# Feed forward's second projection of a three-layer network: seven block products in place of eight

## The reference

```
m = concatenate([a, b]) @ w_out
h = h + rmsnorm(m, post_mix_g)
f = rmsnorm(h, pre_ff_g) @ w_ff1          # 512 x 1024 @ 1024 x 4096
f = square(relu(f)) @ w_ff2               # 512 x 4096 @ 4096 x 1024
h = h + rmsnorm(f, post_ff_g)
```

## Time and profile before

| | us |
|---|---|
| median of 3 runs | 1731.29 |
| lowest, highest | 1729.97, 1731.40 |
| the profiled execution, its time | 1730.73 |
| its span, first to last instruction | 1729.0 |
| PE busy in the span | 1715.3 (99%) |
| VectorE, ScalarE, GpSimd busy | 1209.1, 820.2, 46.4 |

### The profile page before, as it was taken

How to read it: one execution, slowest core, us unless ns; L and a number is a source line. 1 busy time by engine, 2 the same in 40 slices (tenths; PEclk the granted TensorE clock), 3 DMA queues, 4 the chain that set the end, 5 groups by cost and what they waited for, 6 DMA issues and landing times.

```text
span 1729.0 us, 26320 instructions
## 1 busy us (share of the span) xinstructions
PE 1715.3 (99%) x10458; PEld 1497.2 (87%) x10458; DVE 1209.1 (70%) x1975; ACT 820.2 (47%) x1449; POOL 46.4 (3%) x103
## 2 busy tenths in 40 slices
PE   9999999999999999999999999999999999999998
PEld 8777788999999887777989999989888898999997
DVE  4588787777787735666877777868446876677776
ACT  4477744444445235664444444443565555333342
POOL 0212000000000000000000000000000000000000
PEclk9999999999999999999999999999999999999999
DMA  8343332333334232224133333352314224333331
GB/s 276 113 134 118 119 89 87 109 98 110 101 99 153 86 105 84 81 91 122 39 103 98 110 110 97 99 165 82 110 44 140 63 73 126 106 98 98 100 109 49
DMA packets 220125, 181.36 MB, mean 105 GB/s; under 512 B 9906, under 2 KB 178771, under 8 KB 220003
## 3 DMA queue, kind: packets, MB, share of 16 engines
q1 hardware_dynamic: 217954, 175.48, 33.1%
q0 software_dynamic: 2048, 4.20, 0.9%
HBM read 173.32 MB, written 7.38 MB: 105 GB/s over the span
## 4 chain that ended last, share of the span: by engine, by line
PE 93%; DVE 4%; ACT 1%; DMA 1%; issue 1%; POOL 0%; DVEq 0%; POOLq 0%
PE ps L733 29%; PE ps L734 28%; PE ps L735 28%; PE ps L1092 1%; PE ps L1137 1%; PE ps L1163 1%; PE ps L1112 1%; PE ps L1151 1%; DMA arena<-arena 1%; PE ps L987 1%; DVE wlo L1701 0%; DVE xl L1793 0%; PE ps L1102 0%; PE ps L972 0%; ACT whi L1321 0%
## 5 line engine op out<-in xcount | busy, mean ns | idle before, releaser
L1701 DVE TENSOR_TENSOR wlo<-raw,whi 128x1024 fp32r<-128x1024 f32 (+1 forms) x276 | 317.6, 1167 | 181.3 <-ACT whi L1321 181.0
L733 PE MATMUL ps<-xh,whi 128*128 128x256 f32 (+1 forms) x1016 | 332.4, 327 | 2.3 <-DVE xl L1793 2.3
L735 PE MATMUL ps<-xh,wlo 128*128 128x256 f32 (+1 forms) x1016 | 326.1, 321 | 0.0
L734 PE MATMUL ps<-xl,whi 128*128 128x256 f32 (+1 forms) x1016 | 325.9, 321 | 0.0
L1321 ACT ACTIVATE whi<-raw 128x1024 fp32r<-128x1024 f32 (+1 forms) x276 | 274.6, 1007 | 80.9 <-DMA raw<-in_w_ff 36.4
L733 PE MATMUL ps<-whi,hh 128*128 128x512 f32 x728 | 288.7, 397 | 1.4 <-DVE wlo L1701 1.3
L734 PE MATMUL ps<-wlo,hh 128*128 128x512 f32 x728 | 285.2, 392 | 0.0
L735 PE MATMUL ps<-whi,hl 128*128 128x512 f32 x728 | 283.6, 390 | 0.0
L733 PEld LDWEIGHTS ps<-xh,whi 128*128 128x128 f32 x1016 | 194.1, 191 | 25.8 <-issue 8.8
L735 PEld LDWEIGHTS ps<-xh,wlo 128*128 128x128 f32 x1016 | 194.1, 191 | 14.4
L734 PEld LDWEIGHTS ps<-xl,whi 128*128 128x128 f32 x1016 | 194.4, 191 | 12.2
(11 more groups left out here) (272 smaller groups left out, 2935.3 us busy)
## 6 DMA issues: line engine op xcount, KB each, us to landing
raw<-in_ffn_w_in SPq DMA_DIRECT2D x88, 512.0 KB, 3.8
raw<-in_w_ff SPq DMA_DIRECT2D x64, 512.0 KB, 4.2
raw<-in_ffn_w_out SPq DMA_DIRECT2D x44, 512.0 KB, 3.9
raw<-in_a_w_qkv SPq DMA_DIRECT2D x22, 512.0 KB, 5.5
raw<-in_w_in SPq DMA_DIRECT2D x20, 512.0 KB, 3.8
raw<-in_kv_w SPq DMA_DIRECT2D x16, 512.0 KB, 4.1
bias_skewed<-bias_rows SPq DMA_DIRECT2D x8, 640.0 KB
arena<-arena POOLq DMA_DIRECT2D x64, 64.0 KB, 2.7
```

The source lines that it names most:

```text
L733: e.matmul(o, ah, bh, start=start, stop=False, **more)
L734: e.matmul(o, ah, bl, start=False, stop=False, **more)
L735: return e.matmul(o, al, bh, start=False, stop=stop, **more)
L1701: e.tensor_tensor(lo[:, 0:n], src, f32(hi[:, 0:n]), ALU.subtract).then_inc(s.lo, 1)
```

## The change

**The second projection.** Groups 1 to 6 are no longer 16 pieces but a 2 x 2 block product by seven products: tokens in two halves of 256, the four hidden blocks in two halves, outputs in two halves of 512. Each product has two pieces (two token tiles of 128), so a group has 14 pieces. The left operands are three quarters of the hidden blocks as they are and four sums of quarters; the right ones are quarters of the weights and sums of them. Two chains of products run on in PSUM banks that are held: `SEVEN` says for every product which chain it adds to, whether it starts it, and into which token half m and output half nh its running sum is sent, with which sign. After each piece ScalarE copies the bank (times the sign) to one of four buffers, and GpSimd's queue issues a transfer that adds the buffer onto `mb`. PE may add to the bank again when it has been copied.

**Operands.** The hidden blocks of these groups are kept unsplit in the storage of `hh` (`hidden_words`). VectorE makes the left sums, ScalarE the high and VectorE the low part of each left operand, in `left` steps two products ahead. The right operands are loaded by SP into the four buffers of `x`; their sums are made by accumulating transfers from DRAM, issued by GpSimd. `x` is therefore parked in DRAM before and loaded back after. A group has four such sums on right operands and 14 additions onto `mb`.

**Weights.** All weight tiles are laid out in DRAM as the kernel reads them: every load of a tile is 128 contiguous pieces of 4 KB. The right operands have a table of their own, `c_row_tiles`.

**Smaller edits.** `FEED_PIECES` is "2212" in place of "2222". The scratch for GpSimd's transfer descriptors goes from 1024 to 2048. `tri`, the triangle of ones, moves into the arena and is loaded before the gate. The last gain vector has a place of its own, and semaphores with one use are merged into others.

```diff
-FEED_PIECES = ["1111"] + ["2222"] * 13
+FEED_PIECES = ["1111"] + ["2212"] * 13
+SEVEN_FIRST, SEVEN_LAST = 1, 6
+SEVEN = [("a11", 0, True, 0, 0, 1), ("a12", 1, True, 0, 0, 1), ("s1", 1, True, 1, 1, -1), ("s4", 1, False, 0, 1, -1),
+         ("s2", 0, False, 0, 1, -1), ("s3", 0, False, 1, 1, -1), ("a22", 0, False, 1, 0, 1)]
...
+    def seven(self, g):
...
+        rights = [Right(a, ("load", landed), [(a, "a", (first, 1))]), Right(b, ("load", b_need), (), b_next),
+                  Right(a, ("a", 48 * turn + 16), [(a, "a", (last, 1))]),
+                  Right(c, ("load", c_need), [(d, "d", (last, 1))], c_next),
+                  Right(a, ("a", 48 * turn + 32), [(a, "a", (last, 0))]), Right(d, ("d", 16 * turn + 16), (), d_next),
+                  Right(a, ("a", 48 * turn + 48), (), following)]
...
+        for n, (name, chain, start, m, nh, sign) in enumerate(SEVEN):
+            u = 7 * (g - SEVEN_FIRST) + n
+            unit = self.unit("seven", rights[n], None)
+            if g == SEVEN_LAST and n == 6:
+                self.step("gain", self.fifth)
+                self.step("unpark", unit)
+            for t in range(2):
...
+                self.step("seven", piece)
...
+                self.step("seven_post", piece)
+                if t == 1:
+                    self.left(u + 2)
+                yield
...
# PE
+            elif what == "seven":
+                p, = arg
+                b, c = p.bank, slice(p.t * 128, p.t * 128 + 128)
+                wh, wl = self.weight(p.unit, 2)
+                lh, ll = self.left_parts(self.plan.entry_of[p.u])
+                w.wait_ge(s.lo, p.unit + 1)
+                w.wait_ge(s.left_lo, p.u + 1)
+                if p.before is None:
+                    w.wait_ge(*freed[b])
+                else:
+                    w.wait_ge(s.evicted, p.before + 1)
+                for k in (0, 1):
+                    m = mm3(e, ps[b][:], lh[:, k, c], ll[:, k, c], wh[:, k, :], wl[:, k, :], p.start and k == 0, k == 1,
+                            skip_group_check=True)
+                m.then_inc(s.rows, 1)
# ACT
+            elif what == "seven_post":
+                p, = arg
+                w.wait_ge(s.rows, p.value)
+                if p.sent >= 4:
+                    w.wait_ge(s.added[p.sent % 4], 16 * (p.sent // 4))
+                e.activation(self.evict_to(p.sent), ps[p.bank][:], ACT.Copy, scale=float(p.sign)).then_inc(s.evicted, 1)
# DVE
+            elif what == "left_sum":
...
+                if name == "s1":
+                    e.tensor_tensor(tmp, a22, a21, ALU.subtract).then_inc(s.left_sum, 1)
+                elif name == "s2":
+                    e.scalar_tensor_tensor(tmp, tmp, -1.0, a11, ALU.mult, ALU.subtract).then_inc(s.left_sum, 1)
+                elif name == "s4":
+                    e.scalar_tensor_tensor(a12, a12, -1.0, tmp, ALU.mult, ALU.subtract).then_inc(s.left_sum, 1)
+                else:
+                    e.tensor_tensor(a21, a11, a21, ALU.subtract).then_inc(s.left_sum, 1)
# POOL
+            elif what == "split" and self.plan.units[arg[0]][0] == "seven":
+                m, = arg
+                right = self.plan.units[m][1]
+                for buffer, chain, source in right.sums:
+                    if chain == "a":
+                        w.wait_ge(s.lo, m + 1)
+                    else:
+                        w.wait_ge(s.right[buffer], right.before)
+                    e.dma_start(self.x[:, buffer, :], self.row_tile(*source),
+                                accum_op=ALU.add).then_inc(s.right_sum[chain], 16)
+            elif what == "seven_post":
+                p, = arg
+                w.wait_ge(s.evicted, p.sent + 1)
+                w.wait_ge(s.mb, 16)
+                if p.earlier is not None:
+                    w.wait_ge(s.added[p.earlier % 4], 16 * (p.earlier // 4 + 1))
+                e.dma_start(self.mb[:, p.tile, p.nh * 512:p.nh * 512 + 512], self.evict_to(p.sent), accum_op=ALU.add).then_inc(s.added[p.sent % 4], 16)
# SP
+            e.dma_start(self.raw[:, m % RAW, :], ap["c_tiles"][m]).then_inc(s.raw[m % RAW], 16)
...
+            elif what == "park":
+                w.wait_ge(s.add, 8)
+                for t in range(4):
+                    e.dma_start(self.parked[t * 128:t * 128 + 128, :], self.x[:, t, :]).then_inc(s.x, 16)
+            elif what == "seven_load":
+                w.wait_ge(s.x, 128)
+                w.wait_ge(s.y, 16)
+                for buffer, source in ((1, (4, 0)), (2, (6, 0)), (3, (6, 1)), (0, (8, 0))):
+                    rows_load(buffer, source)
...
-    nc = _bacc.Bacc("TRN2", target_bir_lowering=False, num_devices=1, dynamic_dma_scratch_size=1024)
+    nc = _bacc.Bacc("TRN2", target_bir_lowering=False, num_devices=1, dynamic_dma_scratch_size=2048)
```

More of the change, by code:

```diff
@@ L61, in __init__ @@
         self.kind, self.nh, self.t, self.bank, self.i = kind, nh, t, bank, i
-        self.norm, self.group, self.value = norm, group, None
+        self.norm, self.group, self.value, self.added = norm, group, None, None
+class Piece:
+    def __init__(self, u, unit, t, bank, start, before, value, tile, nh, sign, sent, earlier):
+        self.u, self.unit, self.t, self.bank, self.start, self.before, self.value = u, unit, t, bank, start, before, value
+        self.tile, self.nh, self.sign, self.sent, self.earlier = tile, nh, sign, sent, earlier
+class Right:
+    def __init__(self, buffer, need, sums=(), load=None):
+        self.buffer, self.need, self.sums, self.load, self.before = buffer, need, sums, load, None
 class Pair:
-    def __init__(self, kind, n, table, columns, blocks):
+    def __init__(self, kind, n, table, columns, blocks, first=None):
         self.kind, self.table, self.columns, self.blocks = kind, table, columns, blocks
@@ L942, in unsplit @@
             return self.raw[:, tile % RAW, :], 1024
+        if kind == "seven":
+            return self.x[:, tile.buffer, :], 1024
         if kind == "s2":
@@ L1314, in scalar @@
                     w.wait_ge(s.raw[tile % RAW], self.raw_at[tile])
+                elif kind == "seven":
+                    what, value = tile.need
+                    w.wait_ge(s.right[tile.buffer] if what == "load" else s.right_sum[what], value)
                 else:
@@ L1754, in vector @@
                 for i, k in enumerate(pair.blocks):
+                    if pair.kind == "relu":
+                        for n in range(14 * (SEVEN_LAST - SEVEN_FIRST) - 4, 14 * (SEVEN_LAST - SEVEN_FIRST)):
+                            w.wait_ge(s.added[n % 4], 16 * (n // 4 + 1))
                     w.wait_ge(s.hh, pair.hidden[i] + 1)
@@ L2259, in sync @@
                 m, = arg
-                _, _, tile = self.plan.units[m]
+                kind, right, tile = self.plan.units[m]
+                if kind == "seven" and right.load is not None:
+                    w.wait_ge(s.hi, m + 1)
+                    w.wait_ge(s.lo, m + 1)
+                    rows_load(*right.load)
                 if tile is not None and tile + RAW < len(self.plan.tiles):
```

343 lines of the change are left out of this document (244 added, 99 removed).

## The result

| us | before | after |
|---|---|---|
| median of 3 runs | 1731.29 | 1739.84 |
| lowest, highest | 1729.97, 1731.40 | 1736.82, 1743.04 |
| forecast for after | | 1716.0 (1712 to 1729) |

The ratio is 1.0056, with a 95% interval of 1.0042 to 1.0069: the kernel became slower by 0.4 to 0.7%, and the forecast was 24 us too low. The sign was wrong too.

The account below looks back on a forecast made before the run. The prediction took PE's (TensorE's) work to bound the kernel: 1730.73 us less 16.5 for fewer pieces plus 1.5 for entry and exit gives 1715.7, put at 1716 us for the median, range 1712 to 1729.

Parts of the forecast that it names:

- The sign: Whole kernel: faster than before by over 0.2%, under 1727.8 us, chance 0.76.
- PE's work, -16.5 us: Second projection, groups 1 to 6: 14 pieces in place of 16, 2.75 us less per group, 16.5 us in all.
- Accumulate at the copy's price: DMA engines: adding transfers priced like copies, with the tiles 33 to 35 us of a 39.3 us group.
- Rival C: GpSimd's queue and DMA engines, 1430 to 1660 us: accumulating transfers become the bound; 1753 us at 1.5 times copy; chance 0.18.
- I take 0 for the steady state: Groups 1 to 6: engines' queue order costs PE 0 us, bounds 0 and 18 us.
- The wait of 2 us on ScalarE: s2's right operand: its sum takes 8 to 9 us, so ScalarE may stand 2 us, only one eviction behind it.
- Rival B: In-order queues take part back, VectorE and ScalarE waiting on each other: 1722 us, reaching 1719 to 1727.8; chance 0.20.
- Entry and exit, 1.5 together: Parking x, loading right operands and bringing x back: 1.5 us together, bounds 0 and 6.
- Layout 0: Weight tiles in DRAM: shorter landings but no gain, at best the 3.6 us PE waits for low parts.
- Scratch "buys no time that this trace shows": GpSimd's descriptor scratch, enlarged: no time gained that the trace of the kernel before shows.
- GpSimd's issue at 1 us: GpSimd's queue: 1 us to issue each of the 18 accumulating transfers per group.
- VectorE 33.2 and ScalarE 29.4 us per group: Busy time in a 39.3 us group of the second projection: VectorE 84%, ScalarE 75%, neither full.

Follow-up runs that it names:

- e12: Kernel after without its 108 adding transfers, with s3's left sum earlier and the last pair's high parts one step later: 1713.81 us, ratio 0.9905.
- e13: Kernel after with both order moves of e12 and all 108 GpSimd transfers plain, overwriting instead of adding: 1717.71 us, ratio 0.9927.
- e11: e6 with the right operand sum for s2 made by VectorE instead of an adding transfer, whole network computed: 1723.39 us, ratio 0.9958.
- e6: Kernel after, whole network, with s3's left sum earlier and the last pair's high parts one step later on ScalarE: 1731.67 us, ratio 1.0003.
- e15: Kernel after, whole network, with only s3's left sum made earlier, together with those of s2 and s4: 1731.31 us, ratio 1.0003.
- e9: Kernel after in its own order, with none of its 108 adding transfers: 1721.68 us, ratio 0.9949.
- e4: Kernel before with only the weight tiles laid out in DRAM as in the kernel after: 1729.56 us, ratio 0.9997.
- e3: Kernel after without the 84 transfers onto the result, the 24 adding ones on right operands kept: 1726.85 us, ratio 0.9981.
- e8: Kernel after with the descriptor scratch of 1024 as before: 1747.97 us, ratio 1.0101.
- e7: e6 with two right operand sums per group (for s2 and d's operand) made by GpSimd's own addition: 1746.06 us, ratio 1.0086.

## Why the prediction was wrong, point by point

- **PE's work, -16.5 us: right.** e12 and e13 reach 1713.8 and 1717.7 us.
- **"Accumulate at the copy's price": the failed step.** It measured 1.91 times the copy. The 5.8 MB of a group are 32 us of engine time and not the 17 of e13's copies (the forecast had 19 to 21); with 12 to 14 for the tiles that is 44 to 46, the share of 1.05 to 1.09 of the windows. The forecast's 33 to 35 us at the copy's price is near what e13 shows (a share of 0.74 to 0.78, which is 29 to 31 us of 39.3). Rival C had the right factor, by a rule that I cited and gave too small a chance (0.18), but its formula was wrong: it made the period follow the engines' share (1817 us at 2), and e11 has no stall at the same share. The way the price reached PE was the landing of one transfer, 7 to 8 us in place of the 4.1 that I took for it.
- **"I take 0 for the steady state": wrong, 8 us of it order.** The wait of 2 us on ScalarE was foreseen (it was 3.2 to 3.8 in three groups); what stood behind it was not. I listed ScalarE's own queue and left out VectorE's, whose work then came as a burst with s3's left sum last. Rival B named the ping-pong of left sums as what could go wrong, at 6 us; the two causes together, not one of them, make the result slower. Either alone would have left the kernel no slower than before (the adding alone, e6 and e15: equal; the order alone, e9: faster).
- **The half clock was not in the sum at all.** After waits of 2.17, 2.15 and 4.34 us the matmuls ran at the lower level for 3.4, 3.4 and 6.8 us, after one of 2.14 us they did not. That is some 5.5 us of slow starts, a fifth of the loss; with the other slow starts it is 9.8.
- **Entry and exit, 1.5 together: nothing at the entry; the exit is wrong, and beyond the bound of 6.** Even with the order mended the exit loses 10 us in e11; e13 loses about 6 there, 3.3 of it waits. I had counted landings there, but not that the pieces stand closer together and the chain of right sums sets their pace.
- **Layout 0: right (e4). Scratch "buys no time that this trace shows": right by the letter and useless.** It is worth 8 us under the new transfers. GpSimd's issue at 1 us: right (0.94).
- **VectorE 33.2 and ScalarE 29.4 us per group: right and 2 too high.** In e12's five windows from 1450 to 1660 us they are busy 178.0 and 146.1 us of 210, which is 33.3 and 27.3 per 39.3.

## What to carry to other kernels

Price a transfer that adds at twice a copy, both in engine time and, once the engines are full, in landing; then ask not how full the engines are but which engine stands in order for one such landing, and what stands behind it in that engine's queue and in the queues that it feeds. Put work that a burst can delay (here a left sum of 0.7 us) early, and let the sum that is waited for be made by a compute engine with slack, not by GpSimd beside a busy VectorE. Count with PE's waits what follows them: here 17.5 us of waits came with 9.8 us of slow starts.

## What the runs showed of the hardware

- An adding transfer took 1.91 times the engine time per MB of the same transfer as a copy (5.52 and 2.89 us per MB), and at a share of about 0.6 it took 5.95 (e3).
- A reported DMA share of 1.04 to 1.05 went with a completely busy PE (e11): it is no measure of saturation by itself.
- Issuing a transfer of 128 pieces took GpSimd 0.94 us, one of 32 partitions 0.50.
- After waits of PE of 2.17 and 2.15 us the granted clock was 0.50 for 3.4 us each, after waits of 2.14 us (kernel after, and e8) it stayed at 1.00.
- With descriptor scratch 1024 GpSimd stood 50 us in 200 ahead of its issues, with 2048 under 1.
- Beside a GpSimd addition of 128x1024 (2.6 us), a two-input subtraction of VectorE lasted 3.35 us in place of 1.22 (e7).
